# Ten buffers of split weights, each begun 64 bytes further from a multiple of 512

## The chip, the cores and the metric

The program runs on one core of one Trainium2 chip. The metric is the device time of one execution in microseconds. The kernel before was timed three times: 1157.97, 1158.60 and 1158.93 us, a median of 1158.6.

## What is computed

Two small transformer stacks, one after the other, on one sequence of 256 tokens of width 1024, in float32. The first has two layers: an input projection, attention (dilated windows in three groups in the first layer, grouped queries in the second), attention over 256 memory tokens, a gate, and an output projection. The second has two layers: an input projection to 1892 columns, three kinds of attention (a sliding window with sinks, a sparse one chosen by an indexer, a low-rank one), an output projection and a layer norm, then a mixture of 16 experts with two of them chosen for each token, and another norm.

```python
# first stack, layer i
proj = jnp.einsum('bsd,de->bse', rmsnorm(x, norm_g[i]), w_in)
y = jnp.concatenate([o_mix, o_mem], axis=-1) * jax.nn.silu(gate)
x = x + jnp.einsum('bse,ed->bsd', y, w_out[i])
...
# second stack, layer l
x = layer_norm(ALPHA * x + jnp.einsum('bsm,md->bsd', mix, w_out[l]), ...)
h = jax.nn.silu(einsum('nd,edf->enf', xt, w_gate)) * einsum('nd,edf->enf', xt, w_up)
y = jnp.einsum('enf,efd->nd', h * gates, w_down)
x = layer_norm(ALPHA * x + y, ...)
```

Everything large is a product of activations with float32 weights that are read once: some 210 MB of them.

## The kernel before

**Weights in halves and quarters.** The weights come in an order written out by hand, as 198 "halves" of up to 1 MB. The SyncE queue loads them (`sp_load`, L408 to L423) into a ring of three places of 8192 bytes a partition, `ring0` to `ring2`; the experts have two more, `ring_G` and `ring_K`, in memory that is free by then. A load waits until the half that was in its place has been split.

**The split.** A float32 weight is used as the sum of two numbers in TensorE's reduced float32 type, a high and a low part. Each half is split in two "quarters" of 1024 elements a partition: ScalarE copies a quarter to `wH` (`act_cut`, L432), VectorE subtracts that from the quarter and writes `wL` (`dve_cut`, L440). There are five pairs, `wH0`/`wL0` to `wH4`/`wL4`, taken in turn (NQ = 5). A copy into `wH` waits until TensorE has used the quarter five before; TensorE waits until `wL` is written. Activations are split in the same manner: `hTH`/`hTL`, `yTH` with `yTL0` and `yTL1`, `yT2H`/`yT2L`, `xgH`/`xgL`, `gh`.

**The product.** `mm3` (L485 to L489) makes each product of three matmuls: high x high, high x low, low x high. The first argument is the stationary operand (activations, 128 x 128), the second the moving one (weights, mostly 512 columns). TensorE loads a stationary operand for each matmul, while the matmul before is running.

```python
pe.e.matmul(o, a[0], b[0], start=first, stop=False)          # L487
pe.e.matmul(o, a[0], b[1], start=False, stop=False)          # L488
return pe.e.matmul(o, a[1], b[0], start=False, stop=last)    # L489
```

A quarter is mostly two chunks of 512 columns, used for two tiles of 128 tokens: 12 matmuls. In the experts' gate and up projections the chosen tokens fill at most one tile in the path that is run (`pe_few`). The four slabs of each input projection of the second stack (`SPLITS`) are 416, 452, 512 and 512 columns wide; in the narrow ones the second chunk of a quarter begins right behind the first, 1664 or 1808 bytes on. Attention is put between the projections; its transposes and small products are other lines.

**Where things lie.** `sb()` (L141) hands out bytes of a partition one after the other, rounded up to 64, and notes the next free one in `top_of[0]`. The first buffer, `const`, begins at byte 1152 and has 7704 bytes, `rows` 6272, `gcol` 192: so `X` begins at 15360 = 30 x 512. From there to `arena` all sizes are multiples of 512. `arena` has 15136 bytes, so `T0` begins at remainder 320 (of a division by 512); `TA`, `TS`, `mKT`, `mV`, `sm` follow at 320, `factors` (32 bytes) moves `maskR`, `identR` and `zeroR` to 384, and `zeroR` (4 bytes) moves the rings to 448. The ten split buffers of 4096 bytes each come behind the rings, all at remainder 448. Behind them are `mxA`, `denA`, `mx1`, `den1`, `wr`, `few_w`, `SG`, `gT`, `top`, `count` and `slot_gate`, up to byte 225984. A buffer with `at=` lies inside another: `yTL0` in `mKT` (320), `yTL1` in `qkv1` (0), `yT2L` in `T0` (320), `yT2H` in `hTL` (0), `xs`, `OH`, `xgH`, `xgL`, `gh` at 0. `ring_G` is at 0, `ring_K` at 320.

Of the kernel before, what the change touches and what calls it, by code (L numbers as in the profile page):

```python
TOK, D, P = 256, 1024, 128
# [124 lines left out]
def program(nc, t, out, cols, keep):  # L126
# [5 lines left out]
    F32R = mybir.dt.float32r  # L132
# [6 lines left out]
    place, top_of = {}, [(nc.sbuf_base + 63) // 64 * 64]  # L139

    def sb(name, *shape, at=None, dt=F32):  # L141
        size = 4
        for n in shape[1:]:
            size *= n
        if at is None:
            place[name] = top_of[0]
            top_of[0] += (size + 63) // 64 * 64
        else:
            place[name] = place[at[0]] + at[1]
        return nc.alloc_sbuf_tensor_at(name, list(shape), dt, offset=place[name])  # L150
# [56 lines left out]
    NS, NQ = 3, 5  # L207
    ring = [sb(f"ring{i}", P, 2048) for i in range(NS)]
    ring += [sb("ring_G", P, 2048, at=("G", 4096)), sb("ring_K", P, 2048, at=("mKT", 0))]
    NR = len(ring)  # L210
    parts = [[sb(f"w{n}{i}", P, 1024, dt=F32R) for n in "HL"] for i in range(NQ)]
    mxA, denA = sb("mxA", P, 3, 2, 4), sb("denA", P, 3, 2, 4)
    mx1, den1 = sb("mx1", P, 4, 4), sb("den1", P, 4, 4)
    wr = sb("wr", P, 8, 16)
# [139 lines left out]
    for h, (_, srcs) in enumerate(halves):  # L354
        n_places = NR if any(a <= h < b for a, b in more_places) else NS
        i = min(range(n_places), key=lambda x: newest[x])
# [2194 lines left out]
```

## Time and profile before

| | |
|---|---|
| median of three runs | 1158.6 us |
| the profiled execution: its time | 1162.45 us |
| its span, first to last instruction | 1161.1 us |
| TensorE busy | 1118.2 us (96%) |
| VectorE busy | 890.9 us (77%) |
| ScalarE busy | 747.5 us (64%) |
| mean granted clock of TensorE | 0.991 |
| read from HBM | 219.13 MB, 190 GB/s over the span |

PE is TensorE's matmuls, PEld its loads of stationary operands, DVE is VectorE, ACT ScalarE, SP SyncE. Matmuls are pipelined: the duration shown for one (0.39 us) is longer than the distance to the start of the next, and so a run of matmuls is read by their starts. A duration is from one profiled execution.

### The profile page before, as it was taken

The page shows a single profiled execution, that of the slowest core. Times are in us where ns is not written, and L with a number is a line of the kernel's source. Part 1 is how long each engine was busy: PE and PEld are TensorE (multiplying, and loading weights), DVE is VectorE, ACT ScalarE, POOL GpSimd, SP SyncE. Part 2 cuts the span into 40 slices and gives each one's busy share as a digit, 9 for nine tenths or more (in the row PEclk, how much of TensorE's full clock was granted, in tenths as well). Part 3 has the DMA queues.
Part 4 walks back from the last instruction along what each step waited for, and adds up shares of the span by engine and source line. Part 5 has one row for each costly group of instructions (what it writes and reads, how often), then busy time and mean ns, then how long its engine had stood idle before and what let it go on. Part 6 is the DMA issues. An engine that isn't in the chain of part 4 may idle for free.

```text
span 1161.1 us, 14686 instructions
## 1 busy us (share of the span) xinstructions
PE 1118.2 (96%) x5515; PEld 915.6 (79%) x5515; DVE 890.9 (77%) x1476; ACT 747.5 (64%) x1325; POOL 0.2 (0%) x4
## 2 busy tenths in 40 slices
PE   7999999999999999999999999999989999999996
PEld 5788887888787788888878787877778878787774
DVE  4756757777668867767578769999976886999996
ACT  5746565655666665567455557888855655688883
POOL 0000000000000000000000000000000000000000
PEclk9999999999999999999999899999999999999998
DMA  8654454453443454633452416999926332599991
GB/s 290 223 199 145 145 177 137 159 180 110 145 139 116 149 214 151 224 109 134 158 174 80 145 38 208 353 361 362 358 77 233 117 107 76 169 354 355 361 354 40
DMA packets 131844, 221.26 MB, mean 191 GB/s; under 512 B 6145, under 2 KB 77361, under 8 KB 131761
## 3 DMA queue, kind: packets, MB, share of 16 engines
q1 hardware_dynamic: 127920, 213.21, 54.2%
q10 hardware_dynamic: 3840, 6.98, 1.7%
q8 instruction: 47, 0.77, 0.3%
q14 instruction: 37, 0.30, 0.1%
HBM read 219.13 MB, written 1.05 MB: 190 GB/s over the span
## 4 chain that ended last, share of the span: by engine, by line
PE 82%; DVE 10%; ACT 4%; issue 2%; DMA 2%; ACTq 0%; DVEq 0%
PE bank L487 21%; PE bank L489 21%; PE bank L488 21%; PE bank L850 4%; PE bank L786 4%; PE bank L835 2%; DVE wL L440 2%; PE bank L636 1%; DMA ring<-in_w_mem_kv 1%; PE bank L2273 1%; PE bank L2322 1%; ACT wH L432 1%; PE bank L1734 1%; PE bank L2287 1%; PE bank L1795 1%
## 5 line engine op out<-in xcount | busy, mean ns | idle before, releaser
L440 DVE TENSOR_TENSOR wL<-ring,wH 128x1024 fp32r<-128x1024 f32 (+1 forms) x316 | 375.7, 1212 | 132.6 <-ACT wH L432 131.6
L432 ACT ACTIVATE wH<-ring 128x1024 fp32r<-128x1024 f32 (+1 forms) x316 | 320.4, 1047 | 32.8 <-PE bank L489 16.0
L487 PE MATMUL bank<-wH,hTH 128*128 128x512 f32 (+2 forms) x592 | 237.8, 402 | 2.9 <-DVE wL L440 1.9
L488 PE MATMUL bank<-wL,hTH 128*128 128x512 f32 (+2 forms) x592 | 232.0, 392 | 0.0
L489 PE MATMUL bank<-wH,hTL 128*128 128x512 f32 (+2 forms) x592 | 231.8, 392 | 0.0
L487 PEld LDWEIGHTS bank<-wH,hTH 128*128 128x128 f32 x592 | 111.5, 188 | 27.9 <-DVE wL L440 3.4
L489 PEld LDWEIGHTS bank<-wH,hTL 128*128 128x128 f32 x592 | 111.5, 188 | 24.9
L488 PEld LDWEIGHTS bank<-wL,hTH 128*128 128x128 f32 x592 | 111.6, 188 | 22.9 <-issue 0.5
L487 PE MATMUL bank<-wH,xgH 128*128 128x512 f32 x256 | 104.7, 409 | 0.0
L488 PE MATMUL bank<-wL,xgH 128*128 128x512 f32 x256 | 101.2, 395 | 0.0
L489 PE MATMUL bank<-wH,xgL 128*128 128x512 f32 x256 | 101.2, 395 | 0.0
L809 ACT ACTIVATE S<-bank,sm 128x256 f32<-128x256 f32 (+1 forms) x144 | 59.8, 430 | 40.9 <-DVE sm L801 40.8
L841 ACT ACTIVATE PT<-bank 128x512 f32<-128x512 f32 x56 | 31.3, 598 | 41.9 <-PE bank L835 41.9
L487 PEld LDWEIGHTS bank<-wH,xgH 128*128 128x128 f32 x256 | 48.1, 188 | 12.1 <-DVE wL L440 2.6
L489 PEld LDWEIGHTS bank<-wH,xgL 128*128 128x128 f32 x256 | 48.1, 188 | 11.5
L555 ACT ACTIVATE qkv<-bank,factors 128x512 f32<-128x512 f32 x50 | 33.7, 690 | 34.8 <-PE bank L489 34.7
L488 PEld LDWEIGHTS bank<-wL,xgH 128*128 128x128 f32 x256 | 48.2, 188 | 9.5
L487 PE MATMUL bank<-wH,gh 128*128 128x512 f32 x128 | 51.1, 399 | 0.0
L489 PE MATMUL bank<-wH,gh 128*128 128x512 f32 x128 | 50.6, 395 | 0.0
L488 PE MATMUL bank<-wL,gh 128*128 128x512 f32 x128 | 50.6, 395 | 0.0
L440 DVE TENSOR_TENSOR wL<-ring_G,wH 128x1024 fp32r<-128x1024 f32 x40 | 48.5, 1219 | 1.3 <-ACT wH L432 1.0
L440 DVE TENSOR_TENSOR wL<-ring_K,wH 128x1024 fp32r<-128x1024 f32 x40 | 48.2, 1218 | 1.5 <-ACT wH L432 1.4
(296 smaller groups left out, 1864.8 us busy)
## 6 DMA issues: line engine op xcount, KB each, us to landing
ring<-in_w_in_a SPq DMA_DIRECT2D x44, 1024.0 KB, 5.1
ring<-in_w_out SPq DMA_DIRECT2D x20, 1024.0 KB, 4.9
ring<-in_w_down SPq DMA_DIRECT2D x20, 1024.0 KB, 6.4
ring<-in_w_gate SPq DMA_DIRECT2D x36, 512.0 KB, 5.2
ring<-in_w_up SPq DMA_DIRECT2D x36, 512.0 KB, 6.6
ring<-in_w_in_b SPq DMA_DIRECT2D x14, 1024.0 KB, 5.2
ring<-in_w_mem_kv SPq DMA_DIRECT2D x8, 1024.0 KB, 7.8
ring<-in_w_in SPq DMA_DIRECT2D x8, 1024.0 KB, 5.4
```

What stands on the lines that cost most here:

```text
L432: act.e.activation(quarter_parts(q)[0], quarter_in_ring(q), COPY).then_inc(w_high, 1)
L440: dve.e.tensor_tensor(lo, quarter_in_ring(q), hi.bitcast(F32), SUB).then_inc(w_low, 1)
L487: pe.e.matmul(o, a[0], b[0], start=first, stop=False)
L488: pe.e.matmul(o, a[0], b[1], start=False, stop=False)
L489: return pe.e.matmul(o, a[1], b[0], start=False, stop=last)
L555: act.e.activation(dst(i), bank_of["proj", name, i].t[:, 0:slab_w[name]], COPY, scale=factor(key)[:, i:i + 1] if key else 1.0).then_inc(*a ...
L636: tr = pe.e.transpose(o, src(i, j), ident)
L786: mm = pe.e.matmul(score_bank(u, s // each)[:, s % each, :], u.qh(s)[:, i * P:(i + 1) * P], u.kh(s)[:, k:k + n], start=u.mask is None, sto ...
L809: act.e.activation(u.S[:, s, 0:n], score_bank(u, s // each)[:, s % each, :], EXP, bias=nb[:, s:s + 1], scale=u.scale, accum_out=u.den[:, s ...
L835: tr = pe.e.transpose(b.t[:, s * P:(s + 1) * P], u.S[:, s, kt * P:(kt + 1) * P], ident)
L841: act.e.activation(u.PT[:, kt, :, :].rearrange("p h q -> p (h q)"), bank_of["turn", u.name, kt].t[:, :], COPY).then_inc(*act.did("PT", u.n ...
L850: mm = pe.e.matmul(b.t[:, s * u.dv:(s + 1) * u.dv], u.PT[:, kt, s, :], u.vh(s, kt), start=kt + s == 0, stop=kt == u.nk - 1, skip_group_che ...
```

## The change

Behind each of the ten buffers the next free byte is moved on by 64. Buffer k of the ten (wH0, wL0, wH1, ...) begins 64k bytes later than before, and what lies behind all of them 640 bytes later. Nothing else differs.

```diff
-    parts = [[sb(f"w{n}{i}", P, 1024, dt=F32R) for n in "HL"] for i in range(NQ)]
+    parts = []
+    for i in range(NQ):
+        parts.append([])
+        for n in "HL":
+            parts[i].append(sb(f"w{n}{i}", P, 1024, dt=F32R))
+            top_of[0] += 64
     mxA, denA = sb("mxA", P, 3, 2, 4), sb("denA", P, 3, 2, 4)
```

## Rows read from the trace of the kernel before

**Rows 1.** The page's busy line, and the chain that ended last, by line.
```profile
PE 1118.2 (96%) x5515; PEld 915.6 (79%) x5515; DVE 890.9 (77%) x1476; ACT 747.5 (64%) x1325; POOL 0.2 (0%) x4
...
by line: PE bank L487 21.5%; PE bank L489 21.2%; PE bank L488 21.2%; PE bank L850 3.8%; PE bank L786 3.6%; issue 1.9%; PE bank L835 1.7%; DVE wL L440 1.5%; PE bank L636 1.5%; DMA ring<-in_w_mem_kv 1.4%; PE bank L2273 1.2%; PE bank L2322 1.0
```

**Rows 2.** Matmuls at L488: whole span (count in brackets), groups with forms, one by form.
```profile
0.00:1161.00 1161.00, 473.87 (x1200) 227.26 (x1200) 0.99 0.56 191
...
L488 PE MATMUL bank<-wL,hTH x592: 348/394/548, 39.9 to 924.2; 128*128 128x512 f32 x176, 128*128 128x416 f32 x11, 128*128 128x452 f32 x11
...
L488 PE MATMUL bank<-wL,xgH x256: 389/394/398, 707.6 to 1137.0; 128*128 128x512 f32 x128
...
L488 PE MATMUL bank<-wL,gh x128: 391/394/398, 721.2 to 1146.5; 128*128 128x512 f32 x128
...
L488 PE MATMUL bank<-wL,hTH 128*128 128x512 f32 x528 | 208.2, 394 | 0.0
```

**Rows 3.** TensorE's timeline: start, duration, line, tiles; first and last of each run.
```profile
558.07 0.39 PE L487 MATMUL bank<-wH,yTH 128*128 128x512 f32 x1
...
562.97 0.39 PE L487 MATMUL bank<-wH,yTH 128*128 128x512 f32 x1
...
838.31 0.39 PE L487 MATMUL bank<-wH,xgH 128*128 128x512 f32 x1
...
840.88 0.40 PE L489 MATMUL bank<-wH,xgL 128*128 128x512 f32 x1
```

**Rows 4.** TensorE's timeline where the low part begins at remainder 320.
```profile
349.89 0.39 PE L488 MATMUL bank<-wL,yTH 128*128 128x512 f32 x1
...
352.43 0.40 PE L487 MATMUL bank<-wH,yTH 128*128 128x512 f32 x1
...
683.37 0.40 PE L487 MATMUL bank<-wH,yT2H 128*128 128x512 f32 x1
683.61 0.39 PE L488 MATMUL bank<-wL,yT2H 128*128 128x512 f32 x1
683.83 0.39 PE L489 MATMUL bank<-wH,yT2L 128*128 128x512 f32 x1
684.06 0.40 PE L487 MATMUL bank<-wH,yT2H 128*128 128x512 f32 x1
...
685.45 0.40 PE L487 MATMUL bank<-wH,yT2H 128*128 128x512 f32 x1
```

**Rows 5.** TensorE's timeline from 703 us, equal neighbours merged.
```profile
702.63 4.24 PE L2273 MATMUL bank<-OH,xs 128*128 128x512 f32 x18
```

**Rows 6.** TensorE's timeline in a slab 416 columns wide, each third matmul.
```profile
570.00 0.35 PE L487 MATMUL bank<-wH,hTH 128*128 128x416 f32 x1
...
570.58 0.35 PE L487 MATMUL bank<-wH,hTH 128*128 128x416 f32 x1
...
571.13 0.35 PE L487 MATMUL bank<-wH,hTH 128*128 128x416 f32 x1
...
571.71 0.35 PE L487 MATMUL bank<-wH,hTH 128*128 128x416 f32 x1
```

**Rows 7.** Groups by form: the two halves of the split, by ring.
```profile
L440 DVE TENSOR_TENSOR wL<-ring,wH 128x1024 fp32r<-128x1024 f32 x300 | 358.8, 1220 | 116.2 <-ACT wH L432 115.3
...
L440 DVE TENSOR_TENSOR wL<-ring_K,wH 128x1024 fp32r<-128x1024 f32 x40 | 48.2, 1218 | 1.5 <-ACT wH L432 1.4
...
L432 ACT ACTIVATE wH<-ring 128x1024 fp32r<-128x1024 f32 x300 | 305.8, 1053 | 20.0 <-PE bank L489 7.9 <-DMA ring<-in_w_mem_kv 7.9 <-DMA ring<-in_w_in_b 2.0
...
L432 ACT ACTIVATE wH<-ring_K 128x1024 fp32r<-128x1024 f32 x40 | 41.5, 1048 | 0.0
```

**Rows 8.** Windows: busy us and instructions of PE, PEld, DVE, ACT, POOL; PEclk; DMA; GB/s.
```profile
785.00:805.00 20.00, 20.00 (x88) 15.68 (x87) 19.82 (x23) 17.98 (x25) 0.00 (x0) 1.00 1.04 363
...
952.00:954.00 2.00, 2.00 (x12) 1.66 (x11) 1.83 (x8) 2.00 (x10) 0.00 (x0) 1.00 1.11 390
```

**Rows 9.** The same view of one stretch of 100 us.
```profile
600.00:700.00 100.00, 95.91 (x551) 79.21 (x549) 78.11 (x211) 53.86 (x134) 0.00 (x0) 0.97 0.30 98
```

## The prediction

> **What bounds the kernel now.** I read the busy line of the page first, then the chain that ended last, then the costliest groups, then the timeline of TensorE alone, because the change touches addresses and no instruction. The reader is to see in [rows 1] that TensorE is busy for 96% of the span and that three source lines, L487, L488 and L489, hold 21.5 + 21.2 + 21.2 = 63.9% of the chain: 742 of 1161.1 us. These are the three matmuls of `mm3`, and the moving operand of every one is a buffer of split weights (`wH0` ... `wL4`). There are 1200 at each line, 3600 in all. Of the 592 with `hTH` 528 are 512 columns wide and 64 narrower, and no other group has narrow ones [rows 2], so 3 x 1136 = 3408 are 512 wide.
>
> Being "busy" says nothing of the rate, so I measured the rate as the distance between the starts of matmuls that follow one another. In the second layer's output projection 21 intervals take 562.97 - 558.07 = 4.90 us, 233.3 ns each; among the experts 11 intervals take 840.88 - 838.31 = 2.57 us, 233.6 ns [rows 3]. The two stages differ in everything around TensorE and have one interval. I use 233.3. At the full clock, 2.4 GHz, one column a cycle would be 213 ns (my estimate of the floor), so some 20 ns of each interval are something else, and no idle time stands beside them.
>
> **Does the interval depend on where operands start?** From the sizes in the code, `const` begins at byte 1152 of a partition; `hTH`, `hTL`, `yTH`, `S`, `Y`, `G` and `arena` begin at a multiple of 512 (remainder 0), `T0` to `sm` at remainder 320, the rings and all ten split buffers at 448. The timeline has three cases with other remainders.
> - The low part of `yT` lies at remainder 320 for its first four chunks (`yTL0`) and at 0 for the rest (`yTL1`). Same lines, same tiles, same moving operands: with `yTL1` the 233.3 above; with `yTL0` 11 intervals take 352.43 - 349.89 = 2.54 us, 230.9 ns [rows 4]. For `yT2L`, also at 320, 9 intervals take 2.08 us, 231.1 ns [rows 4]. One of three stationary operands is moved, and the mean of the three falls by 2.3 ns. Written out they are uneven: 0.24, 0.22, 0.23 us.
> - L2273 multiplies `OH` by `xs`, both at remainder 0. Eighteen matmuls take 4.24 us to the end of the last one [rows 5]; less its own 0.39 us (as in [rows 3]), 3.85 / 17 = 226.5 ns.
> - Against: in the slabs 416 columns wide the second chunk of a buffer begins 1664 bytes on, at remainder 64. Three matmuls at 64 take 0.58 us, the next three at 448 0.55 us, the next three at 64 0.58 us again, and so on in turn [rows 6]. Remainder 64 is slower than 448 there, by 0.03 us in three or up to 10 ns a matmul; each start is rounded to 0.01 us, so it may be as little as 3, and over the whole slab, where the pair is repeated, I take 4.
>
> So something in TensorE's operand reads depends on starts, by several ns of 233, in either direction. The Trainium skill, page "SBUF — State Buffer", section "Who interferes with whom", gives TensorE two independent read ports and has it wait on nobody; no start address comes into it, and by it the sum of this change would be zero. The trace differs: 231 against 233 ns at the same lines.
>
> **The change part by part.** No instruction, wait or transfer is added or removed.
> - *The ten buffers.* Buffer k (wH0, wL0, wH1, ...) moves by 64k bytes. The remainders become 448, 0, 64, 128, 192, 256, 320, 384, 448, 0. `mm3` reads the high part twice and the low part once; over the five pairs that is 15 reads, of which wH0 and wH4 keep 448 in four: 11 of 15 are changed. The price per matmul is what no row shows for a whole set of remainders. The bounds are 6.8 ns gained (233.3 - 226.5) and 4 ns lost. I take the 2.3 ns of the `yTL0` rows as the mean over all, since they are the nearest: same tiles and same lines, with the relation of the two operands altered for part of the three. Of it 742 / (3408 x 0.2333 + 192 x 0.2) = 742 / 833 = 0.89 lies on the chain. 3408 x 2.3 ns x 0.89 = 7.0 us.
> - *ScalarE writes wH, VectorE writes wL.* If their reads and writes cared for remainders, the rings would show it: from `ring` (448) and `ring_K` (320) VectorE takes 1220 and 1218 ns, ScalarE 1053 and 1048 ns [rows 7]. I book nothing. A real 3 ns on 396 pieces of VectorE would be 1.2 us, on an engine that TensorE hides except where it lets TensorE wait.
> - *Everything behind them* (`mxA` to `slot_gate`) moves by 640 bytes: small operands, in the router's and the softmax's few-element instructions. The rings lie before the buffers and stay, so no transfer has another target. Nothing booked; the cover is TensorE's queue of projections.
> - *Who is next when TensorE is faster.* Among the experts VectorE is busy 19.8 of 20 us and the DMA engines' share is over 1.0 at 363 GB/s [rows 8]. The experts hold 3 x (256 + 128) of the matmuls [rows 2]; at 2.3 ns each they ask for 1% more. Transfers have run at 390 GB/s in a busy stretch [rows 8], 7% above, so I book the full gain.
>
> Sum: the profiled execution's 1162.45 us (span 1161.1 and 1.35 around it) becomes 1155.4; the median of the runs shown lies 3.85 lower, so 1158.6 - 7.0 = 1151.6.
>
> **The rivals.**
> - *Full gain.* All changed remainders behave as the pair at L2273: 6.8 ns x 3408 x 11/15 x 0.89 = 15.1 us, 1143.5. For: the one pair with another relation in steady state has it. Against: with eight different remainders it would be luck if all were good, and [rows 6] show a bad one.
> - *No effect.* The interval is set by something else and the `yTL0` rows owe their 2.3 ns to the stationary operand alone, which this change leaves at 0; or good and bad remainders cancel. 1158.6. For: the 233.3 and 233.6 of two very different stages. The page of the Trainium skill cited above would be on this side, with 1158.6.
> - *Slower.* Remainder 448 is a good one, as in [rows 6], and the rest lose 4 ns: 4 x 3408 x 11/15 x 0.89 = 8.9 us, 1167.5. One mechanism, in the moving operand's read; it decides as soon as the mean interval is above 233.3. For: those are the only rows in which the moving start itself differs with everything else the same. Against: these matmuls are 416 wide, and where their read ends differs too.
> - *The gain is there but capped.* The experts' stages are held by VectorE or by transfers: 1152 / 3408 of 7.0 us, 2.4 us, is not had; 1154.0. For: 19.8 of 20 us. Against: no idle time of TensorE there.
>
> **How the numbers follow.** Forecast 0.42 (own range, intervals of 229 to 232.4 ns: 3 to 13 us, 1145.5 to 1155.8); full gain 0.1; no effect 0.2; slower 0.2; capped 0.08. Within 0.2%, 2.3 us, is about what a measurement of this kernel can tell from no change. The forecast and its two kin give faster 0.58, with 0.02 of the forecast's low end falling to "same"; same 0.22; slower 0.20. The range 1143.5 to 1165.0 leaves out half of the slower case and the far side of the full gain.
>
> **What the changed profile would show.** The starts of the 512-wide matmuls: a mean of about 231 ns in the same stretches, now differing from buffer to buffer, with 448 (wH0, wH4) as before. Busy time of L440 and L432 at 1218 to 1220 and near 1050 ns. The chain's share of L487 to L489 near 742 - 7 us, the attention stages' waits as now. In the 416-wide slabs other remainders, other intervals. Wrong would be: intervals of 233.3 everywhere; a mean above it; VectorE or ScalarE with other durations by buffer; or faster matmuls and a DMA wait among the experts. Apart from the addresses one thing can move a few us: TensorE's mean granted clock is 0.97 in one stretch of 100 us [rows 9], so it ran at 1.2 instead of 2.4 GHz for some 6 us of it; one such fall more or less is up to 3 us.

## The result

The changed kernel takes 1158.12 us (median of 20 runs, 1154.48 to 1161.05), the kernel before, run beside it, 1162.82 us (20 runs, 1157.74 to 1165.63). The ratio is 0.9964, with a 95% interval of 0.9954 to 0.9975: faster by 0.36%, 4.2 us. The forecast was 7.0 us. (The 1158.6 us of the three runs shown first lie at the low end of what the kernel before does; the ratio counts.)

### The profile after

The page's busy line, the chain by line, and the groups that answer to [rows 1], [rows 2] and [rows 7]. The lines have moved by five: `mm3` is at L492 to L494, the split at L445 and L437.

```profile
PE 1113.1 (96%) x5515; PEld 915.7 (79%) x5515; DVE 891.1 (77%) x1476; ACT 747.6 (65%) x1325; POOL 0.2 (0%) x4
...
by line: PE bank L492 21.5%; PE bank L493 21.1%; PE bank L494 21.1%; PE bank L855 3.9%; PE bank L791 3.4%; issue 1.9%; PE bank L840 1.6%; PE bank L2278 1.5%; PE bank L641 1.5%; DVE wL L445 1.3%; ACT wH L437 1.3%; DMA ring<-in_w_in_a 1.3%; P
...
L493 PE MATMUL bank<-wL,hTH x592: 346/395/401, 39.0 to 919.7; 128*128 128x512 f32 x176, 128*128 128x416 f32 x11, 128*128 128x452 f32 x11
...
L493 PE MATMUL bank<-wL,xgH x256: 387/392/628, 704.1 to 1134.5; 128*128 128x512 f32 x128
...
L445 DVE TENSOR_TENSOR wL<-ring,wH 128x1024 fp32r<-128x1024 f32 x300 | 358.9, 1220 | 116.7 <-ACT wH L437 115.8
...
L445 DVE TENSOR_TENSOR wL<-ring_K,wH 128x1024 fp32r<-128x1024 f32 x40 | 48.3, 1219 | 1.4 <-ACT wH L437 1.4
...
L437 ACT ACTIVATE wH<-ring 128x1024 fp32r<-128x1024 f32 x300 | 306.0, 1053 | 20.3 <-PE bank L494 7.8 <-DMA ring<-in_w_mem_kv 7.2 <-DMA ring<-in_w_in_a 2.7
...
L437 ACT ACTIVATE wH<-ring_K 128x1024 fp32r<-128x1024 f32 x40 | 41.5, 1048 | 0.0
```

The reader is to see that TensorE is busy for 5.1 us less (1113.1 after 1118.2), that VectorE's and ScalarE's pieces cost what they did within 1 ns, and that the three lines of `mm3` are 63.7% of the chain, 63.9% before. The duration shown of one matmul (its middle value, in ns) is no guide: 395 against 394. The stretches that answer to [rows 3] (first two pairs), [rows 4] (next two pairs) and [rows 6] (last four rows), in TensorE's timeline of the changed kernel:

```profile
556.59 0.40 PE L492 MATMUL bank<-wH,yTH 128*128 128x512 f32 x1
...
561.47 0.39 PE L492 MATMUL bank<-wH,yTH 128*128 128x512 f32 x1
...
835.54 0.39 PE L492 MATMUL bank<-wH,xgH 128*128 128x512 f32 x1
...
838.07 0.40 PE L494 MATMUL bank<-wH,xgL 128*128 128x512 f32 x1
...
348.82 0.40 PE L493 MATMUL bank<-wL,yTH 128*128 128x512 f32 x1
...
351.37 0.39 PE L492 MATMUL bank<-wH,yTH 128*128 128x512 f32 x1
...
678.50 0.39 PE L492 MATMUL bank<-wH,yT2H 128*128 128x512 f32 x1
...
680.58 0.40 PE L492 MATMUL bank<-wH,yT2H 128*128 128x512 f32 x1
...
568.47 0.35 PE L492 MATMUL bank<-wH,hTH 128*128 128x416 f32 x1
...
569.04 0.35 PE L492 MATMUL bank<-wH,hTH 128*128 128x416 f32 x1
...
569.61 0.35 PE L492 MATMUL bank<-wH,hTH 128*128 128x416 f32 x1
...
570.18 0.35 PE L492 MATMUL bank<-wH,hTH 128*128 128x416 f32 x1
```

The 21 intervals take 4.88 us, 232.4 ns each (233.3 before); the 11 among the experts 2.53 us, 230.0 ns (233.6 before); with `yTL0` 2.55 us for 11, 231.8 ns (230.9 before: slower now); with `yT2L` 2.08 us for 9, 231.1 ns as before. In the narrow slab the chunks that took 0.58, 0.55 and 0.58 us take 0.57 each.

To see the whole trace and not stretches, I took all distances between the starts of two `mm3` matmuls that follow one another, 512 columns wide, of 200 to 260 ns (3105 to 3138 in each trace; longer ones have a wait or other work in them). Their mean is 233.15 ns before and 231.75 ns after. This mean stands as "mean interval" in what follows.

The same matmuls, by their starts in [rows 3] and [rows 4] and above, run ahead of before by 1.48 us at 558 us, by 4.87 us at 683 us, and by 2.77 us at 838 us. By the addresses alone the lead should only grow; that it jumps and falls back goes with the clock. The windows view of both kernels, the kernel before first (columns as in [rows 8]):

```profile
650.00:660.00 10.00, 9.10 (x29) 6.81 (x30) 6.91 (x20) 5.05 (x15) 0.00 (x0) 0.66 0.84 264
711.00:717.00 6.00, 5.92 (x35) 4.79 (x33) 5.52 (x17) 3.62 (x6) 0.00 (x0) 1.00 0.67 188
```

and the changed kernel:

```profile
650.00:660.00 10.00, 10.00 (x60) 8.12 (x59) 8.61 (x26) 5.93 (x20) 0.00 (x0) 1.00 1.03 319
711.00:717.00 6.00, 6.00 (x24) 4.87 (x25) 5.55 (x8) 2.40 (x4) 0.00 (x0) 0.72 0.65 200
```

Before, TensorE ran at half its clock for part of the stretch from 650 to 660 us, and at full clock from 711 to 717 us. After, it is the other way round, and TensorE is busy without a gap in both stretches. A mean clock of 0.66 over 10 us is 6.8 us at 1.2 instead of 2.4 GHz, which costs 3.4 us, the jump of the lead from 558 to 683 us. One of 0.72 over 6 us is 3.4 us at the lower clock; the changed kernel has another such stretch from 694.9 to 698.3 us (granted clock 0.50), and the two together cost 3.4 us, more than the 2.1 us by which the lead falls back. Ahead of the fall in the kernel before TensorE was busy 9.54 of 10 us from 640 to 650 us and 1.40 of 2.30 us from 650 to 652.3 us, at a granted clock of 1.00. Both traces have more such falls, at places that differ from trace to trace. They go with the spread of the runs: among the 20 runs of the changed kernel the quickest (1154.48 us) has a mean granted clock of 0.993, the slowest (1161.05 us) one of 0.988; 0.005 of 1158 us is 5.8 of their 6.6 us.

### The profile page after: what moved, and what is told of

It is laid out like the page before. It is cut to its first block, busy times and chain, and to the rows that moved or that the text cites. A ratio compares the mean times of both kernels' runs of the same rounds, so it can differ in the third digit from the quotient of the medians.

```text
span 1158.3 us, 14686 instructions
## 1 busy us (share of the span) xinstructions
PE 1113.1 (96%) x5515; PEld 915.7 (79%) x5515; DVE 891.1 (77%) x1476; ACT 747.6 (65%) x1325; POOL 0.2 (0%) x4
## 4 chain that ended last, share of the span: by engine, by line
PE 82%; DVE 9%; ACT 5%; issue 2%; DMA 2%; ACTq 0%; DVEq 0%
PE bank L492 21%; PE bank L493 21%; PE bank L494 21%; PE bank L855 4%; PE bank L791 3%; PE bank L840 2%; PE bank L2278 2%; PE bank L641 1%; DVE wL L445 1%; ACT wH L437 1%; DMA ring<-in_w_in_a 1%; PE bank L2327 1%; PE bank L1739 1%; PE bank L2292 1%; PE bank L1800 1%
## 5 line engine op out<-in xcount | busy, mean ns | idle before, releaser
L445 DVE TENSOR_TENSOR wL<-ring,wH 128x1024 fp32r<-128x1024 f32 (+1 forms) x316 | 375.5, 1212 | 131.8 <-ACT wH L437 130.8
L437 ACT ACTIVATE wH<-ring 128x1024 fp32r<-128x1024 f32 (+1 forms) x316 | 320.4, 1047 | 32.0 <-PE bank L494 14.9
L492 PE MATMUL bank<-wH,hTH 128*128 128x512 f32 (+2 forms) x592 | 237.6, 401 | 3.8 <-DVE wL L445 2.8
L493 PE MATMUL bank<-wL,hTH 128*128 128x512 f32 (+2 forms) x592 | 231.1, 390 | 0.0
L494 PE MATMUL bank<-wH,hTL 128*128 128x512 f32 (+2 forms) x592 | 230.6, 389 | 0.0
L492 PEld LDWEIGHTS bank<-wH,hTH 128*128 128x128 f32 x592 | 111.2, 188 | 28.1 <-DVE wL L445 4.3
L494 PEld LDWEIGHTS bank<-wH,hTL 128*128 128x128 f32 x592 | 111.2, 188 | 24.3
L492 PE MATMUL bank<-wH,xgH 128*128 128x512 f32 x256 | 105.7, 413 | 0.0
L494 PE MATMUL bank<-wH,xgL 128*128 128x512 f32 x256 | 101.9, 398 | 0.0
L492 PEld LDWEIGHTS bank<-wH,xgH 128*128 128x128 f32 x256 | 48.9, 191 | 12.5 <-DVE wL L445 3.1
L494 PEld LDWEIGHTS bank<-wH,xgL 128*128 128x128 f32 x256 | 48.8, 191 | 11.3
L492 PE MATMUL bank<-wH,gh 128*128 128x512 f32 x128 | 50.9, 398 | 0.0
L494 PE MATMUL bank<-wH,gh 128*128 128x512 f32 x128 | 50.3, 393 | 0.0
L445 DVE TENSOR_TENSOR wL<-ring_G,wH 128x1024 fp32r<-128x1024 f32 x40 | 48.5, 1220 | 1.2 <-ACT wH L437 1.0
L445 DVE TENSOR_TENSOR wL<-ring_K,wH 128x1024 fp32r<-128x1024 f32 x40 | 48.3, 1219 | 1.4 <-ACT wH L437 1.4
```

The source lines that it names most:

```text
L437: act.e.activation(quarter_parts(q)[0], quarter_in_ring(q), COPY).then_inc(w_high, 1)
L445: dve.e.tensor_tensor(lo, quarter_in_ring(q), hi.bitcast(F32), SUB).then_inc(w_low, 1)
```

## The experiments

Two theories stood at the start. **Theory A**: the interval of a matmul is set by how far its moving operand begins from the stationary operands, modulo 512. **Theory B**: a common start is as good as any other, and the gain comes from neighbours that differ. They part in a kernel whose ten buffers all have one remainder: by A the time depends on which, by B it is that of before for any. A third, **C**, holds with A that 448 is itself among the good values. Every kernel below is the kernel before with nothing but free bytes put in, so no instruction differs. Ratios are to the kernel before on the same chip, with their 95% intervals; "by intervals" is (233.15 - mean interval) x 3408 x 0.89, the prediction's own formula, set against 1162.3 us, the median of before beside the first of them. "High" is wH, "low" wL; where nothing else is said the stationary operands are at 0, but for `yTL0` and `yT2L` at 64 (320 by a division by 512).

| kernel | remainders of the ten, mod 256 | mean interval, ns | ratio by intervals | ratio measured |
|---|---|---|---|---|
| before | 192 | 233.15 | 1 | 1 |
| the change | 192/0, 64/128, 192/0, 64/128, 192/0 | 231.75 | 0.9963 | 0.9964 (0.9954 to 0.9975) |
| all_at_0 | 0 | 228.17 | 0.9870 | 0.9903 (0.9871 to 0.9935) |
| all_at_64 | 64 | 229.48 | 0.9904 | 0.9928 (0.9902 to 0.9955) |
| all_at_192 | 192 | 233.17 | 1.0001 | 0.9994 (0.9974 to 1.0015) |
| all_at_320 | 64 | 229.34 | 0.9901 | 0.9907 (0.9874 to 0.9941) |
| all_moved_64 | 0, stationary at 64 | 233.13 | 0.9999 | 0.9991 (0.9969 to 1.0013) |
| all_at_128 | 128 | 232.61 | 0.9986 | 0.9983 (0.9964 to 1.0002) |
| all_at_32 | 32 | 233.09 | 0.9998 | 1.0001 (0.9982 to 1.0020) |
| all_at_224 | 224 | 233.11 | 0.9999 | 0.9992 (0.9973 to 1.0011) |
| high_192_low_0 | high 192, low 0 | 233.82 | 1.0017 | 0.9998 (0.9976 to 1.0021) |
| high_0_low_64 | high 0, low 64 | 231.94 | 0.9968 | 0.9953 (0.9933 to 0.9974) |
| pairs_in_step | 192, 0, 64, 128, 192 | 231.88 | 0.9967 | 0.9965 (0.9948 to 0.9983) |
| all_starts_at_0 | 0, all stationary at 0 | 227.92 | 0.9864 | 0.9848 (0.9821 to 0.9874) |

The measured ratios carry the clock with them: the mean granted clock of a kernel's runs is not quite that of the runs of before beside them, and 0.001 of it goes with about 0.1% of the time, as in the 20 runs above. My estimate of the ratio at an equal clock is therefore the measured one plus the difference of the clocks: 0.9886 for all_at_0 (0.9888 against 0.9905), 0.9874 for all_starts_at_0 (0.9923 against 0.9897), 0.9972 for high_0_low_64 (0.9916 against 0.9897), 0.9981 for pairs_in_step (0.9913 against 0.9897) and 1.0018 for high_192_low_0 (0.9926 against 0.9906).

### A common remainder: 0, 64, 192, 320

One line ahead of the list of buffers, with 64, 128, 256 or 384 in it:

```diff
+    top_of[0] += 64
     parts = [[sb(f"w{n}{i}", P, 1024, dt=F32R) for n in "HL"] for i in range(NQ)]
```

> All ten buffers of split weights begin at remainder 0 of 512 (64 bytes further than before), none of them apart from the others. Theory A (the distance of the moving operand's start from the stationary's, modulo 512, sets the interval): the pair is then that of OH and xs, so a uniform interval near 226.5 ns against 233.3, 6.8 ns x 3408 x 0.89 = 20 us less, ratio 0.982. Theory B (what changed the time is that neighbouring buffers begin at different remainders; a common one is as good as any other): 233.3 ns, ratio 1.000. Theory C (448 is among the best remainders and the change gained only by chance of a few): intervals of 233 or more, ratio 1.000 to 1.005.

> All ten buffers at remainder 64 (128 bytes further than before). Theory A: its own uniform interval, not 233.3; by the buffer at 64 in the changed kernel (wH1, mean 231.7 ns) some 231.7, 1.6 x 3408 x 0.89 = 5 us less, ratio 0.996; by the 416-wide rows of before 237, ratio 1.010. Theory B: 233.3 ns, ratio 1.000.

> All ten buffers at remainder 192 (256 bytes further than before). Theory A: an interval of its own, by wH2 of the changed kernel (mean 231.3 ns) 6 us less, ratio 0.995. Theory B: 233.3 ns, ratio 1.000.

> All ten buffers at remainder 320 (384 bytes further than before). Theory A: an interval of its own, by wH3 of the changed kernel (mean 231.2 ns) 6 us less, ratio 0.995. Theory B: 233.3 ns, ratio 1.000. The intervals where the stationary low part lies at 320 too (yTL0, yT2L) then tell whether the distance of the two starts counts (they would equal those of remainder 0 with stationary 0) or the moving start alone.

Theory B falls: common remainders of 0, 64 and 320 are faster than before and have shorter intervals than the mixture, and 192 is the kernel before. Theory C falls too, since 0 is faster than 448. Theory A holds with another period: 192 behaves as 448, and 64 as 320, so what counts is the remainder of 256, not of 512. The timeline of all_at_0 in the stretch of [rows 3] (here `mm3` is at L488 to L490):

```profile
549.70 0.39 PE L488 MATMUL bank<-wH,yTH 128*128 128x512 f32 x1
...
551.06 0.39 PE L488 MATMUL bank<-wH,yTH 128*128 128x512 f32 x1
...
553.10 0.39 PE L488 MATMUL bank<-wH,yTH 128*128 128x512 f32 x1
...
554.46 0.39 PE L488 MATMUL bank<-wH,yTH 128*128 128x512 f32 x1
```

The nine intervals between the second and the third of these rows take 2.04 us, 226.7 ns, near the 226.5 of [rows 5]; over the stretch of 21 it is 554.46 - 549.70 = 4.76 us, 226.7 ns. The mean over the trace is 228.17, for two reasons. An interval settles only over several matmuls: in all_starts_at_0 the first three after the long one (290 to 340 ns) that follows a wait are 231.4, 231.7 and 232.5 ns in the mean over 133 such runs of matmuls, and from the tenth on they are 226.6 to 227.0. And the stretches with `yTL0` and `yT2L` still have unlike starts in all_at_0 (all_starts_at_0, where these are moved too, has 227.92). The forecasts for 64 and 320 from the changed kernel's own buffers (231.7 and 231.2 ns) were too high by 2 ns: there they stood among unlike neighbours. What all_at_320 was to tell by the stretches with `yT2L` stays mixed: one of three operand pairs has the distance 0 there and two have 64, and the mean is 231.7 ns against 229.2 with `hTH`/`hTL`, as unlike neighbours have it below.

### Distance or place?

```diff
+    top_of[0] += 64
     X = sb("X", P, 2, D)
```

> 64 bytes are left free ahead of X, so that every buffer from X on begins 64 bytes further: the split buffers at 0 of 512, hTH, xgH and all that were at 0 now at 64. The moving starts are those of the kernel with all ten at 0, the distances to the stationary starts those of the kernel before. Theory A1 (the distance of the two starts counts): the interval of before, 233.3 ns, ratio 1.000. Theory A2 (the moving start alone counts): 228.1 ns as with all ten at 0, ratio 0.990.

Here the stationary operands are moved too, so that the moving ones begin where those of all_at_0 do and the distance is that of before. In the same stretch:

```profile
555.32 0.39 PE L488 MATMUL bank<-wH,yTH 128*128 128x512 f32 x1
...
560.21 0.40 PE L488 MATMUL bank<-wH,yTH 128*128 128x512 f32 x1
```

The 21 intervals take 4.89 us, 232.9 ns, much as in [rows 3] (233.3). So it is a distance between starts that counts and not where the moving operands lie. That the other end of it is the stationary operand this run alone doesn't show, since all that lies behind `X` moves with it, the rings too. The `yTL0` and `yT2L` rows of [rows 4], where only a stationary operand begins elsewhere, point to it. So do the means of all matmuls with `yT2H`/`yT2L`: 231.1 ns in all_at_0, where the low part begins at 320, and 229.4 in all_starts_at_0, where it begins at 0. The rings are excluded: they begin at 448 in all_at_0 and at 128 in all_starts_at_0, and both settle at 226.7 ns.

### The other remainders

> All ten buffers at remainder 128 of 512. If the period is 256 and not 512 (192 equals 448, and 64 equals 320, in the four kernels before), 128 is the one class of the four multiples of 64 not yet seen. Theory A: an interval of its own between the best and the worst seen, 227 to 233.3 ns; by wL1 and wL3 of the changed kernel, which lie there, about 229.8, ratio 0.993. Theory of a smooth curve 228.1, 229.3, x, 233.3: 231, ratio 0.995.

> All ten buffers at remainder 32. Theory A with a smooth dependence: between 228.1 (at 0) and 229.3 ns (at 64), ratio 0.991 to 0.992. If the unit of the dependence is smaller than 64 bytes it may lie outside; the 452-wide matmuls that begin at 16 of 256 in the kernel with all ten at 0 have 203.0 ns against 204.8 at 0, so up to 2 ns less than 228.1, ratio 0.985.

> All ten at remainder 224 of 256, 32 bytes below a multiple of 256. If a remainder of exactly 0 is the special one and its neighbours are not (32 above it: 233.2 ns): 233 ns, ratio 1.000. If the good region reaches to 0 from below: 228 to 231 ns, ratio 0.988 to 0.995.

The edits are those of all_at_0 with 192, 96 and 288. A distance of 128 gives 232.6 ns; 32 and 224 (that is, 32 short) give 233.1. The good distances are 0 and, less so, 64; the hope for 32 drawn from the 452-wide rows was a miss, and what a distance of 0 gives is gone 32 bytes to either side. The curve is not smooth: 32 has none of the gain that lies on both sides of it.

### High and low unlike

The mixture's 231.75 ns should now be the mean of its classes. Theory D says that unlike starts of the high and the low buffer cost something of their own; theory E that a change of start from one quarter to the next does so too.

```diff
+    ahead_of, parts = (0, 64, 192, 64, 192, 64, 192, 64, 192, 64), []
+    for i in range(NQ):
+        parts.append([])
+        for n in "HL":
+            top_of[0] += ahead_of[2 * i + "HL".index(n)]
+            parts[i].append(sb(f"w{n}{i}", P, 1024, dt=F32R))
```

with (64, 64, 192, 64, ...) for high_0_low_64 and (0, 0, 64, 0, 64, 0, 64, 0, 64, 0) for pairs_in_step.

> The five high buffers at remainder 192 of 256 (as before), the five low ones at 0. Theory A with each matmul paying for its own buffer alone: (2 x 233.3 + 228.1) / 3 = 231.6 ns, 1.7 x 3408 x 0.89 = 5 us less, ratio 0.9955. Theory D (an interval also depends on the start before it, and differing starts in one triple cost something of their own, which is where the change lost part of its gain): more than 231.6; by wH0, wL0 of the changed kernel, which lie so, (2 x 232.7 + 235.7) / 3 = 233.7, ratio 1.001.

> The five high buffers at remainder 0, the five low ones at 64: the two best common remainders, unlike within each triple. Each matmul paying for its own buffer alone: (2 x 228.1 + 229.3) / 3 = 228.5 ns, ratio 0.988. Theory D (unlike starts in a triple cost something of their own; 2.2 ns a matmul with 192 and 0): 230.7 ns, ratio 0.993 to 0.995.

> The high and the low buffer of a pair begin at the same remainder of 256, the five pairs at 192, 0, 64, 128 and 192 (in the changed kernel it is 192/0, 64/128, 192/0, 64/128, 192/0). Theory A+D (each remainder has its interval, and a cost of its own arises only where high and low differ within a triple): the mean of the common-remainder kernels, (233.3 + 228.1 + 229.3 + 232.6 + 233.3) / 5 = 231.3 ns, ratio 0.995. Theory E (the cost of differing starts arises between quarters too, since the intervals settle over many matmuls): above 231.3, up to 233, ratio 0.995 to 1.000.

The stretch of [rows 3] in high_192_low_0:

```profile
558.10 0.40 PE L492 MATMUL bank<-wH,yTH 128*128 128x512 f32 x1
...
563.02 0.40 PE L492 MATMUL bank<-wH,yTH 128*128 128x512 f32 x1
```

4.92 us for 21 intervals, 234.3 ns: longer than before (233.3), though a third of the reads now has the best distance. If each matmul paid for its own buffer alone, the mean over the trace would be (2 x 233.2 + 228.2) / 3 = 231.5 ns here and (2 x 228.2 + 229.4) / 3 = 228.6 ns in high_0_low_64; they have 233.8 and 231.9. So unlike starts cost 2.3 and 3.3 ns, and theory D stands. In the times the first of the two is a tie (0.9998) and the second is faster, 0.9953. pairs_in_step, with equal starts inside each pair, has 231.88 ns where the mean of its classes is (2 x 233.2 + 228.2 + 229.4 + 232.6) / 5 = 231.3: 0.6 ns are lost where quarters with unlike starts meet, as theory E has it, a small cost in the mean. It keeps steps from pair to pair but none inside a pair, and comes out as the change does (0.9965 and 0.9964).

The trace of the changed kernel shows where its own loss sits, if its matmuls are sorted by the pair they read (intervals inside a quarter, 512 columns wide, without the `yT` and `yT2` stretches). The pairs at 64 and 128 have 230.9 and 230.7 ns, about the mean of their classes (230.5). Of the three at 192 and 0, wH2/wL2 and wH4/wL4, which follow a pair at 64 and 128, have 231.8 and 231.6 ns, the mean of their classes (231.5); only wH0/wL0, which follows wH4/wL4, a pair like itself, has 234.3. In high_192_low_0, where every pair follows one like itself, all five have 234.2 to 234.6 ns, wH0/wL0 as the others, so its place is not the reason. The cost of unlike starts builds up: in the quarters of twelve matmuls the first three intervals of wH2/wL2 and wH4/wL4 are 229.9 and 229.4 ns in the mean, the last three 234.4 and 234.1. One pair with 2.8 ns too much is 0.56 ns in the mean of five.

### Everything at a common remainder

```diff
+    top_of[0] += 192
     T0 = sb("T0", P, 2, 1024)
...
+    top_of[0] += 384
     parts = [[sb(f"w{n}{i}", P, 1024, dt=F32R) for n in "HL"] for i in range(NQ)]
```

> All ten split buffers at a multiple of 256 and, with 192 bytes ahead of T0, also T0, mKT and all others that hold a stationary low part (yT2L, yTL0): every pair of operands of mm3 has distance 0. The 152 + 48 or so intervals of the two output projections that were at 229 to 233 ns come down to 227 or 228: against the kernel with the ten at 0 alone 1 us less at most; against before 228.0 ns, ratio 0.989 to 0.990. If the distance of 64 on one stationary operand does no harm: the same as with the ten at 0 alone, 0.990.

The first line moves `T0` and what follows it from remainder 320 to 0, with `yTL0` and `yT2L` in them, the second the ten buffers. The stretch that answers to `yT2L` in [rows 4] (here `mm3` is at L489 to L491), seven starts that follow one another:

```profile
671.32 0.39 PE L489 MATMUL bank<-wH,yT2H 128*128 128x512 f32 x1
671.54 0.39 PE L490 MATMUL bank<-wL,yT2H 128*128 128x512 f32 x1
671.77 0.39 PE L491 MATMUL bank<-wH,yT2L 128*128 128x512 f32 x1
672.00 0.39 PE L489 MATMUL bank<-wH,yT2H 128*128 128x512 f32 x1
672.23 0.39 PE L490 MATMUL bank<-wL,yT2H 128*128 128x512 f32 x1
672.45 0.39 PE L491 MATMUL bank<-wH,yT2L 128*128 128x512 f32 x1
672.68 0.39 PE L489 MATMUL bank<-wH,yT2H 128*128 128x512 f32 x1
```

Six intervals take 1.36 us, 226.7 ns, against 231.1 before and after the change. The ratio is 0.9848 (0.9821 to 0.9874), 1145.29 us beside 1164.09: faster than the kernel before by 1.5% and than the change by some 1.2%. The ratio by intervals, 0.9864, lies inside; at an equal clock (above) it would be nearer 1.3%. That the kernel is also faster than all_at_0 the two ratios' intervals don't settle, since they touch (0.9871 and 0.9874).

## Why the prediction was right or wrong

- **What bounds the kernel: right.** The ratio by intervals, the prediction's formula with the measured mean, lies inside the measured interval for 12 of the 13 other kernels and 0.0001 outside it for all_at_0. The factor 0.89 for the share on the chain holds to within that; for the kernels that gain most it gives a little too much, as the last point says.
- **The term that was mis-sized: "I take the 2.3 ns of the `yTL0` rows as the mean over all".** It measured 1.4 ns (233.15 to 231.75), and 1.4 x 3408 x 0.89 = 4.2 us is the gain that was measured. Two steps under it failed. The period was taken as 512, with "11 of 15 are changed"; it is 256, where 192 and 448 are one class, so wH2 is unchanged as well and 6 of 15 reads gain nothing. With the kernels of one remainder as prices the mixture is (6 x 233.2 + 3 x 228.2 + 4 x 229.4 + 2 x 232.6) / 15 = 231.1 ns, a gain of 2.1 ns, 6.3 us: near the forecast. The second step is that each matmul was priced by its own operands. Its neighbours count too, which the uneven 0.24, 0.22 and 0.23 us of [rows 4] had hinted at. The rest of the shortfall, 0.6 ns or 1.9 us, is the net of unlike starts, and nearly all of it lies in one pair: wH0/wL0, which follows a pair with the same two starts, has 234.3 ns where its classes have 231.5. The two other pairs at 192 and 0 come behind a pair at 64 and 128 and are through before the cost has built up.
- **"Something in TensorE's operand reads depends on starts": right**, more exactly on the distance between them (all_moved_64). Fourteen traces of one instruction stream have means from 227.9 to 233.8 ns. The Trainium skill, page "SBUF — State Buffer", section "Who interferes with whom", has TensorE's two read ports wait on nobody and names no start address; read as "starts cost nothing" it differs from these traces, and the measurement decides.
- **The 416-wide rows as the case against: read rightly, wrongly carried over to another width.** In [rows 6] remainder 64 is slower than 448, by 3.7 ns in the trace (0.572 against 0.561 us for three matmuls); in matmuls 512 wide it is faster by 3.7 ns (all_at_64). The rival "slower", built on it, has no case among the common remainders: none is above 233.2 ns. Only an unlike pair is (233.8), and its time is a tie.
- **The full-gain rival** priced its best row rightly: settled intervals of all_at_0 have 226.7 ns for its 226.5. It wrongly took the other distances to be as good.
- **ScalarE and VectorE: right.** 1220, 1219, 1053 and 1048 ns after, within 1 ns of [rows 7]. Sorted by buffer, VectorE's pieces have means of 1219.5 to 1220.1 ns over the five `wL`.
- **The cap among the experts: not in the change, but it is there for the kernels that gain more.** The time for one expert, a mean over twelve between like instructions, is 8.75 us before and 8.70 after, which is the whole gain: 36 matmuls of 1.4 ns less are 0.05 us. In all_starts_at_0 it is 8.64, a gain of 0.11 us where 36 matmuls of 5.2 ns less are 0.19. No idle time of PE shows, since the durations of its matmuls overlap, but its weight loads wait for VectorE's `wL`. Over eight experts of the second layer (us in total, times, longest), in before, the change and all_at_0:

```profile
PEld bank L487 <- DVE wL L440: 0.9, 4, 0.3
...
PEld bank L492 <- DVE wL L445: 1.0, 4, 0.4
...
PEld bank L488 <- DVE wL L441: 1.3, 4, 0.4
```

VectorE is busy 19.8 of 20 us there in the changed kernel, as before:

```profile
785.00:805.00 20.00, 20.00 (x90) 15.71 (x89) 19.83 (x24) 17.30 (x25) 0.00 (x0) 1.00 1.03 369
```

So the rival's mechanism is real, with VectorE as the holder, and its price is near nothing at a gain of 1.4 ns; at one of 5.2 ns 0.08 us an expert, 2.6 us over the 32, are not had. The waits above have grown by some 0.05 us an expert of it.

## What to carry to other kernels

Where TensorE is the bound and its matmuls are like these (float32r, 512 columns, a weight load each), read the distance between their starts and not the busy share: by the prediction's estimate 20 ns of each 233 were neither columns nor a wait, and 64 free bytes in one place (all_at_0) took 5 of them. Begin the moving and the stationary operands at the same remainder of a division by 256, all buffers of a rotation alike; tried here with both at 0, while a common remainder other than 0 for all of them was not. Spreading the buffers over remainders, as one might against conflicts, is the wrong cure here: it averages over good and bad distances and can pay for unlike neighbours besides. And look at the engine behind: a gain of 5 ns a matmul already met VectorE among the experts. When the cause is a distance, try each value by itself, as one rotation's buffers in a common place, before pricing a mixture from single rows.

## What the runs showed of the hardware

- The interval of 512-column float32r matmuls, each with a stationary load of its own, by the distance of the operands' starts modulo 256 bytes: 0: 228.2 ns, 32: 233.1, 64: 229.4, 128: 232.6, 192: 233.2, 224: 233.1. Settled, a distance of 0 has 226.7 ns. What in the chip does this no run tells.
- An interval also depends on the matmuls before it, over about a quarter of twelve: the same two buffers' starts, 192 and 0, have 231.6 to 231.8 ns behind a pair at 64 and 128 and 234.3 behind a pair like themselves.
- In settled stretches the stage around the matmuls makes no difference: in an output projection and among the experts it is 233.3 and 233.6 ns before [rows 3], 226.7 and 226.4 ns in all_at_0 in the same two stretches (4.76 us / 21, and 2.49 us / 11).
- At 416 columns the order of two distances is the other way round, 448 before 64 [rows 6]. The traces of the common remainders hold these matmuls too, two starts 128 apart in turn: settled, three matmuls take 0.57 us at 64 and 128 and 0.56 us at 0 and 192 (all_at_0, all_at_64, all_at_128, all_at_192). Both chunks together take 1.13 us in each, so at this width a common remainder gained nothing. No kernel had one distance alone at this width.
- TensorE's granted clock falls from 2.4 to 1.2 GHz for some us (6.8 from 652.3 to 659.1 us before, 3.4 from 694.9 to 698.3 us after) at places that differ between the traces. The mean granted clock goes with most of the spread between runs of one kernel: 5.8 of 6.6 us between the quickest and the slowest of the changed kernel's 20.
